# Four buffers in place of eight in the ring of fetched expert rows

## What is computed

```python
act = gelu(einsum('tkd,td->tk', peer_u[e], ub))          # k = 8 heads x 16 experts
out = einsum('tk,tkd->td', gate * act, peer_v[e])
```

## Time and profile before

| | us |
|---|---|
| median of three runs | 6682.14 |
| lowest, highest | 6679.54, 6698.62 |
| profiled execution, its own time | 6678.65 |
| its span, first to last instruction | 6676.6 |
| TensorE busy | 5486.7 (82%) |
| VectorE busy | 3833.7 (57%) |
| POOL busy | 1875.6 (28%) |
| ScalarE busy | 1192.3 (18%) |

### The profile page before, as it was taken

The page is one execution under the profiler, slowest core; times in us unless marked ns, Lnnn a source line. Parts: engine busy times, 40 slices in busy tenths (PEclk is TensorE's granted clock), DMA queues, the critical chain, the costliest instruction groups (busy, mean ns, idle before and its releaser), DMA issues.

```text
span 6676.6 us, 62677 instructions
## 1 busy us (share of the span) xinstructions
PE 5486.7 (82%) x22755; PEld 3635.5 (54%) x22755; DVE 3833.7 (57%) x8953; ACT 1192.3 (18%) x2559; POOL 1875.6 (28%) x1700
## 2 busy tenths in 40 slices
PE   8899877868757779999997899887786668788876
PEld 3699454735554334554552489744655555455554
DVE  1554163737267898876674355342737376766555
ACT  1100032221373000000002110021312450000001
POOL 0000000000487564554551000000001584444442
PEclk9899978778856889999998889899567768898988
DMA  6000101012115999999995200001012249999996
GB/s 210 14 1 1 38 1 32 1 32 63 64 76 238 387 397 389 387 392 358 387 389 206 86 1 1 13 26 32 1 32 64 79 173 374 349 367 369 359 347 245
DMA packets 290066, 1165.07 MB, mean 175 GB/s; under 512 B 24416, under 2 KB 106592, under 8 KB 205024
## 3 DMA queue, kind: packets, MB, share of 16 engines
q0 software_dynamic: 92160, 671.13, 24.9%
q1 hardware_dynamic: 192272, 441.96, 18.9%
q10 hardware_dynamic: 5328, 47.99, 1.7%
HBM read 1116.94 MB, written 44.04 MB: 174 GB/s over the span
## 4 chain that ended last, share of the span: by engine, by line
PE 63%; DMA 13%; DVE 13%; ACT 5%; issue 4%; POOL 1%; ACTq 0%; DVEq 0%; SPq 0%; POOLq 0%
PE psum L413 63%; DMA weight_ring<-in_ut 12%; DVE arena L1261 3%; ACT y_features L975 2%; ACT arena L903 2%; DVE arena L1540 1%; DVE arena L1615 1%; DVE arena L1270 1%; DVE arena L1264 1%; DVE u_features L1267 1%; DVE x_tokens L1261 1%; DVE arena L1382 1%; DVE arena L1267 0%; ACT y_features L977 0%; DVE arena L1357 0%
## 5 line engine op out<-in xcount | busy, mean ns | idle before, releaser
L413 PE MATMUL psum<-u_features,weight_ring 128*128 128x256 f32 (+2 forms) x6464 | 2014.4, 471 | 345.3 <-DMA weight_ring<-in_ut 313.8
L413 PEld LDWEIGHTS psum<-u_features,weight_ring 128*128 128x128 f32 x6464 | 1312.0, 205 | 1074.3 <-DMA weight_ring<-in_ut 361.8
L413 PE MATMUL psum<-weight_ring,consts 128*128 128x512 f32 x2560 | 1141.8, 593 | 2.6 <-DMA weight_ring<-in_uv 1.9
L413 PE MATMUL psum<-arena 128*128 128x64 f32 (+5 forms) x7136 | 983.5, 320 | 45.5 <-DVE arena L1540 23.9
L413 PEld LDWEIGHTS psum<-arena 128*128 128x128 f32 (+2 forms) x7136 | 842.1, 218 | 131.2 <-issue 32.1
L1248 POOL DMA_INDIRECT arena<-in_uv,arena x560 | 833.4, 1488 | 160.4 <-POOL arena L1244 87.2
L413 PEld LDWEIGHTS psum<-weight_ring,consts 128*128 128x128 f32 x2560 | 484.8, 190 | 540.6 <-issue 491.2
L1762 DVE SCALAR_TENSOR_TENSOR y_features<-arena,y_features 128x1024 f32<-128x1024 f32 x560 | 718.0, 1282 | 12.0
L1747 DVE CUSTOM_DVE_ANT_0 arena<-arena,y_features 128x1024 f32<-128x1024 f32 x560 | 665.1, 1219 | 36.7 <-DMA arena<-in_uv,arena 36.6
L1244 POOL TENSOR_TENSOR arena<-consts 128x1 f32<-128x1 f32 x320 | 343.4, 1073 | 1148.5 <-DVE y_features L1762 1125.9
L1230 POOL TENSOR_SCALAR y_features<-consts 128x128 f32<-128x128 f32 x640 | 525.8, 838 | 463.1 <-ACT consts L965 267.7
(11 more groups left out here) (194 smaller groups left out, 5123.1 us busy)
## 6 DMA issues: line engine op xcount, KB each, us to landing
weight_ring<-in_ut SPq DMA_DIRECT2D x256, 512.0 KB, 8.8
weight_ring<-in_uv SPq DMA_DIRECT2D x256, 512.0 KB, 8.6
weight_ring<-in_ws SPq DMA_DIRECT2D x234, 512.0 KB, 3.6
gate_blocks<-arena ACTq DMA_DIRECT2D x20, 2048.0 KB, 6.3
consts<-gate_blocks SPq DMA_DIRECT2D x16, 768.0 KB, 17.3
arena<-gate_blocks SPq DMA_DIRECT2D x16, 768.0 KB, 18.3
arena<-in_uv,arena POOLq DMA_INDIRECT x560, 10.4
consts<-gate_blocks SPq DMA_DIRECT2D x16, 512.0 KB, 15.5
```

The costliest lines, as they stand in the source:

```text
L413: return pe.matmul(o, w, x, start=first, stop=last, skip_group_check=True)
```

## The change

One constant is halved. RING falls from 4 to 2, so that POOL may be two groups ahead of VectorE's sums in place of four. Buffers 4 to 7 aren't used any more by the ring, and the semaphores and the columns of DOT, GEL and WGT of these buffers go too. The number, size and order of the gathers, and all other instructions, stay.

```diff
-GSLOTS = 8
+GSLOTS = 4
 GROUP = 2
 RING = GSLOTS // GROUP
 GROUPS = TOPK // GROUP
```

## The result

The changed kernel takes 6883.55 us (median of 4 runs, 6877.75 to 6898.92) against 6685.14 us before on the same chips: ratio 1.0297, 95% interval 1.0273 to 1.0322, some 198 us slower. The forecast was 6973 us, its range 6775 to 7240. The profiled executions took 6877.75 and 6678.65 us.

The account below looks back on a forecast made before the run. DMA was 0.92 to 1.00 busy in the five gather stretches; TensorE set layer 0 tiles 2 and 3's pace, late up weights held layer 1. Terms summed to +291 us on 6678.65, 6970, plus 3.5 to the median: 6973 us, range 6775 to 7240.

Parts of the forecast that it names:

- The loop of sum, issue, landing, dot and sum over two groups: In the five gather stretches, two such loops interleave, so a group costs at least half of one, about 8.3 to 8.9 us.
- a: Time from the end of VectorE's sum to POOL's issue of the second gather, taken as 2.9 us.
- b: Time from the second gather's issue to the landing of its row, taken as 9.0 us.
- c: Time from the second dot's start to the sum's end, 5.6 us with routing, 4.6 without, 5.8 in layer 1's first tile.
- Tile 1, +109: Layer 0's first tile: 64 groups at 8.8 us, 563 us for 454, so +109 us.
- Tile 2, +60: Layer 0's second tile: 563 us for 503, so +60 us, the bound moving from TensorE to the loop.
- Tile 3, +22: Layer 0's third tile, without routing: 64 groups at 8.3 us, 531 us for 509, so +22 us.
- Gate blocks, +38: Layer 0's 32 gate fetches, 3.8 us each, lengthen the loop in flight; a third counted, +38 us.
- Layer 1, +62: Layer 1's two tiles: 32 pairs without a stall grow 3.9 us each, 125 us; half taken, +62 us.
- the third rival: Layer 1's up weights come sooner, half of TensorE's 205.7 us waiting goes: -103 us, 6579 us; chance 0.05.
- the strict reading of the rule: Each gather waits out a VectorE instruction locking the port: sum to second issue stays 3.43 us, some 60 us more.
- Landing by the estimate of 4.4 us: The skill's 2.0 us fixed plus bytes over 436 GB/s for a 1 MB row; the loop would be 12.9 us.

## Why the prediction was right, and where its sizes were off

- **The loop of sum, issue, landing, dot and sum over two groups** is right. Distance two with eight buffers gives the whole loss, at distance one every second row is used as it lands and a group takes a + b + c, and distance three, where the loop would not bind, costs nothing.
- **Tile 1, +109:** +104.9. Its 8.8 us a group were 8.74, partly by errors that cancel: a 2.5 for 2.9, b 9.2 for 9.0.
- **Tile 2, +60:** +87.7. The term mis-sized is b, 10.2 for 9.0 us, (10.2 - 9.0)/2 x 64 = +38, less a's -11.
- **Tile 3, +22:** +37.2, again b, 9.9.
- **Gate blocks, +38:** no run isolates them. What a group took beyond half its measured loop is 0.17, 0.08 and 0.05 us in the three tiles, 19 us in all, so outside b they can't have cost more. That layer 0 came to +229.8 against a forecast of +229 with them is luck. The measured b is worth some 75 us more than the 9.0 of the forecast over the three tiles, the measured a some 38 us less than its 2.9, and what is left is about the 38 put down for gate blocks. (The five windows that the forecast names, 560 to 620 us, leave these 38 us out.)
- **Layer 1, +62:** -13.6, and -5.5 and -4.3 in the two other traces with distance two. This is the step that failed, the half that I took of 125 us. (The 125 took the first tile's loop of 17.7 us for both; with the second's 16.5 it would be 106.) I held the stalls on weights to be fixed but for what slower pairs would give back. In fact all of its matmuls' waiting for up weights went, the 205.7 us that the third rival named as its price, and the loop took back about as much: 193.3 us of waiting for gelu in its place. The rival's mechanism was there and its place was right; what it had wrong was that half would go, and its doubt, that the engines were already 0.92 to 0.94 busy, was mine too. They came to 0.94 and 0.96. Of the 92 us by which the forecast lies above the difference of the profiled executions, 76 are layer 1's and 17 the stretches outside the windows.
- **Term a,** and the rule on the port (Trainium skill, SBUF — State Buffer, "SBUF: two separate sides"). POOL's multiply averaged 0.70 us after in place of 1.07, and a was 2.5: nearer to the idle end than to the strict reading of the rule. The runs with release by row and without the multiply agree with it in kind: an issue moved beside a VectorE instruction is stretched, to 1.7 and 1.4 us on average for 1.1. That a port is the cause no run shows.
- **Landing by the estimate of 4.4 us** (Trainium skill, DMA: Bandwidth & Descriptors, "Anatomy of one DMA — SWDGE (gpsimd) path"): the least landing in any tile of the changed kernel is 5.3 us, and the second row of a lone pair takes 7.8. The measurement decides; with 4.4 us from issue to landing the change would have cost nothing. But these times count from the start of POOL's issuing instruction, 0.94 us at the least. Counted from its end, the least landing is 4.3 us in the changed kernel and, with rows of half the size, 3.1 us. So the estimate is about right for a row that waits for nothing and leaves out the issue itself and what the other row and the weights add.
- **What the profile was to show.** VectorE's waits for rows: 841.6 us, where I expected 300 to 500. They took over its former waits for ScalarE and for gate blocks as well, so their sum says little about the loss. The median landing of both rows together was 8.3, 9.0, 8.9, 9.2 and 9.2 us by tile, near the 9 that I named; the second row alone, which counts, was 9.2 to 10.6 on average. TensorE's waits moved to ScalarE's gelu of blocks, 193.3 us, and not to VectorE's weighted blocks, 12.6 us. DMA share fell to 0.86 and 0.88 as expected in tiles 1 and 2, but not in layer 1.

```profile
L1747 DVE CUSTOM_DVE_ANT_0 arena<-arena,y_features 128x1024 f32<-128x1024 f32 x640 | 782.4, 1225 | 843.6 <-DMA arena<-in_uv,arena 841.6
L1244 POOL TENSOR_TENSOR arena<-consts 128x1 f32<-128x1 f32 x320 | 222.4, 695 | 1725.5 <-DVE y_features L1762 1702.6
```

- **Outside the windows, nothing forecast:** -18.5 us between the layers' gathers. A stretch outside the windows that changes was named as a sign of being wrong, but it isn't the ring's: in the fourteen traces of all kernels this stretch took 1880.6 to 1902.3 us in no order of the distance, and 1902.3 and 1901.9 with distance two in layer 1 alone and with four buffers released by row, as much as the 1901.9 of before. Within the 18.5, 2.9 are explained: TensorE no longer lags behind VectorE at the end of layer 0, so VectorE goes on 6.1 us after its last sum in place of 9.0. 9.3 us come from one stretch of layer 1's mixer, the same 186 instructions of VectorE in both kernels, with a lower granted clock before (before, then after):

```profile
4744.50:4815.80 71.30, 68.47 (x406) 57.08 (x405) 52.09 (x186) 18.69 (x25) 0.00 (x0) 0.58 0.00 1
```

```profile
4970.60:5032.60 62.00, 57.07 (x386) 47.73 (x385) 50.60 (x186) 18.64 (x25) 0.00 (x0) 0.69 0.00 1
```

Why the clock rose sooner there isn't settled. The rest, some 6 us, is spread over the mixer.

## What to carry to other kernels

Size a ring by its loop: free to issue, issue to landing of the last piece, landing to free again; with distance n a step costs at least an n-th of it, and beyond that point more buffers bring nothing. Read the landing of the last piece of a group, not the median of all, and release each buffer by itself when the ring is tight. Where a prefetch shares the DMA engines with transfers that are needed sooner, a deeper ring can cost time: try shorter distances stage by stage, with each buffer released by itself. In layer 1 distance two with that release was the fastest tried, though its loop binds.

## What was not expected of the hardware

- Less run-ahead moved the same bytes faster: in layer 1 the rate rose from 365 and 350 GB/s (distance four) to 383 and 392 (distance two by row, without the multiply). Distance two alone left them at 355 and 370; the release by row brought them to 375 and 389, and at distance three by row layer 1 lay in between. So both have a share in it. That the cause is an even spacing of the gathers between the weights was only argued.
- Taking away seven eighths of the weights' bytes shortened a gather's landing by only 0.7 to 1.7 us of 9 to 10.6, while halving the gather's own bytes took off 2.9 to 3.3 us.
- POOL's one-column multiply takes 0.19 us with VectorE idle and 1.1 beside a dot, and a gather's issue 0.94 against 1.66 us, so work taken from POOL's path is partly given back.
